# A tile that outlives its stage receives the next stage's first weight piece, and GpSimd clears the convolution input

## The reference, cut to what matters

```python
def first_block(x, c, ctx, c_ctx, ...):
    mx = split(silu(c) @ w_ada + b_ada, 6)          # shifts, scales and gates for the tokens
    mc = split(silu(c_ctx) @ w_ada + b_ada, 6)      # and for the 256 context tokens
    hx = modulate(rms_norm(x, g_pre_mix), mx[0], mx[1])
    hc = modulate(rms_norm(ctx, g_pre_mix), mc[0], mc[1])
    # token mixer: one projection (q, k, v, o, gates, ga, gb); a bidirectional mLSTM over q, k, v;
    # a depthwise convolution of width 31 over u = ga * sigmoid(gb); both @ w_out
    yx = token_mixer(hx, hc, w_in, ..., w_out)
    x = x + mx[2] * rms_norm(yx, g_post_mix)
    x = x + mx[5] * rms_norm(moe_ffn(...), g_post_ffn)      # 64 experts, 8 of them per token, one shared
    return x

def second_block(x, ...):
    for layer in range(2):
        h = rms_norm(x, norm[layer])
        x = x + (even_mixer(h, w_in, w_out) if layer == 0 else diff_mixer(h, w_qkv, ..., w_out))
        x = x + conv_ffn(rms_norm(x, ffn_norm[layer]), w_up[layer], conv_w, conv_b, w_down[layer])
    return rms_norm(x, final_norm)
```

## Time and profile before

| | |
|---|---|
| runs (median of three) | 2587.68 us (2585.64 to 2591.24) |
| profiled execution | 2594.0 us, its span 2592.2 us, around it 1.8 us |
| mean granted TensorE clock | 0.951 |
| busy PE, PEld | 2358.1 us (91%), 1759.2 us (68%) |
| busy DVE, ACT, POOL | 1536.8 us (59%), 1174.2 us (45%), 298.9 us (12%) |
| pieces of `w_in`, issue to landing, median | 3.2 us (20 of 512 KB) |
| pieces of `w_out`, issue to landing, median | 4.8 us (8 of 512 KB) |
| parts of the attention weights, issue to landing, median | 6.7 and 6.2 us (3 of 512 KB, twice) |
| quarters of the first `w_up` piece, issue to landing, median | 4.3 us (8 of 256 KB) |

### The profile page before, as it was taken

The page is one execution under the profiler, slowest core; times in us unless marked ns, Lnnn a source line. Parts: engine busy times, 40 slices in busy tenths (PEclk is TensorE's granted clock), DMA queues, the critical chain, the costliest instruction groups (busy, mean ns, idle before and its releaser), DMA issues. The chain is left out here.

```text
span 2592.2 us, 30584 instructions
## 1 busy us (share of the span) xinstructions
PE 2358.1 (91%) x10686; PEld 1759.2 (68%) x10686; DVE 1536.8 (59%) x2415; ACT 1174.2 (45%) x1853; POOL 298.9 (12%) x222
## 2 busy tenths in 40 slices
PE   6998887899999999982899789999989979999997
PEld 2875674576776776752666568888757757788886
DVE  3974445677777777748454447637536544674663
ACT  3314342566666666643354434324324533442341
POOL 0000000111211211220343000000014410000000
PEclk9997888999999999996999899999989999999999
DMA  6303424699999999956421212222232211323222
GB/s 241 104 25 123 147 74 166 235 360 359 351 356 357 358 353 354 375 214 239 162 73 41 74 67 96 93 102 97 82 130 73 66 29 52 130 89 103 89 85 72
DMA packets 87041, 427.39 MB, mean 165 GB/s; under 512 B 19760, under 2 KB 19888, under 8 KB 51344
## 3 DMA queue, kind: packets, MB, share of 16 engines
q1 hardware_dynamic: 67632, 392.32, 41.5%
q0 software_dynamic: 19296, 33.60, 3.6%
HBM read 415.36 MB, written 38.80 MB: 175 GB/s over the span
## 5 line engine op out<-in xcount | busy, mean ns | idle before, releaser
L1772 DVE TENSOR_TENSOR w_gu_low<-raw,w_gu_high 128x1024 fp32r<-128x1024 f32 x264 | 322.8, 1224 | 120.7 <-ACT w_gu_high L1721 106.8
L1721 ACT ACTIVATE w_gu_high<-raw 128x1024 fp32r<-128x1024 f32 x264 | 279.8, 1061 | 107.6 <-PE banks L1677 106.8
L2672 PE MATMUL banks<-h_high,w_high 128*128 128x512 f32 x704 | 275.8, 392 | 14.5 <-DVE w_low L2772 14.5
L2672 PE MATMUL banks<-h_low,w_high 128*128 128x512 f32 x704 | 275.3, 391 | 0.0
L2672 PE MATMUL banks<-h_high,w_low 128*128 128x512 f32 x704 | 275.3, 391 | 0.0
L1689 PE MATMUL banks<-raw,act_t 128*128 128x512 f32 x528 | 237.6, 593 | 0.9 <-ACT act_t L1744 0.9
L1677 PE MATMUL banks<-w_gu_high,x_t_high 128*128 128x512 f32 x528 | 213.5, 404 | 2.0 <-DVE x_t_low L1779 2.0
L1677 PE MATMUL banks<-w_gu_high,x_t_low 128*128 128x512 f32 x528 | 207.5, 393 | 0.0
L1677 PE MATMUL banks<-w_gu_low,x_t_high 128*128 128x512 f32 x528 | 207.1, 392 | 0.0
L2699 ACT ACTIVATE w_high<-raw 128x2048 fp32r<-128x2048 f32 (+2 forms) x74 | 124.1, 1676 | 156.4 <-PE banks L2682 152.7
L2736 DVE TENSOR_TENSOR w_low<-raw,w_high 128x2048 fp32r<-128x2048 f32 (+2 forms) x74 | 148.3, 2004 | 58.7 <-ACT w_high L2699 58.6
(11 more groups left out here) (443 smaller groups left out, 4710.6 us busy)
## 6 DMA issues: line engine op xcount, KB each, us to landing
raw<-in_w_e SPq DMA_DIRECT2D x198, 1024.0 KB, 9.5
raw<-in_w_up SPq DMA_DIRECT2D x42, 1024.0 KB, 4.8
w_ada<-in_w_ada_later SPq DMA_DIRECT2D x16, 1024.0 KB, 5.0
expert_rows<-y_rows SPq DMA_DIRECT2D x16, 1024.0 KB, 11.5
raw<-in_w_down SPq DMA_DIRECT2D x16, 768.0 KB, 4.2
w_qkv<-in_w_even SPq DMA_DIRECT2D x7, 1536.0 KB, 6.4
w_qkv<-in_w_odd SPq DMA_DIRECT2D x7, 1536.0 KB, 6.8
w_in<-in_w_in SPq DMA_DIRECT2D x20, 512.0 KB, 3.2
```

What stands on the lines that cost most here:

```text
L1721: act.activation(w_gu[c].high[:].rearrange("p j n -> p (j n)"), ex.chunk(c, s), ACT.Copy).then_inc(gu_high, 1)
L1772: dve.tensor_tensor(w_gu[c].low[:].rearrange("p j n -> p (j n)"), ex.chunk(c, s), w_gu[c].high[:].rearrange("p j n -> p (j n)").bitcast(F3 ...
L2672: mm = pe.matmul(ps[:, 2 * s + c, :], wp[:, at:at + P], hp[:, k, :], start=(k == 0 and i == 0), stop=(k == KT - 1 and i == 2))
```

## The change

A class `Early` holds one tile of 512 KB with a semaphore of its own, opened outside the stages; `fetch` asks for a transfer into it and counts, `now` gives the semaphore's value after the last one. Each of eight stages finds its first piece there, asked for by the stage ahead. Where the stage has a ring of four `raw` buffers, the early tile takes the place of the first. ACT and DVE treat the first piece ahead of the slices of `h`, where they did it after some. `u` is cleared by GpSimd. In `mlstm` the last eight rows reuse the place of the first eight. One `Early` serves from `prologue` to `mixer_out` and is closed after it, a second one serves from `combine` to the end.

```diff
+class Early:
+
+    def __init__(self, sb, sem):
+        self.tile, self.arrived, self.asked = sb("early", [P, KT * P]), sem("early_in"), 0
+
+    def fetch(self, sp, src):
+        sp.dma_start(self.tile[:], src).then_inc(self.arrived, 16)
+        self.asked += 1
+
+    def now(self):
+        return 16 * self.asked
...
                 sp.dma_start(m.rowv[:], d["rowv"]).then_inc(rowv_in, 16)
+                m.early.fetch(sp, d["w_in"][0])
                 sp.wait_ge(rowv_in, 16)
...
-        raw = [sb(f"w_in{s}", [P, KT * P]) for s in range(RAW)]
+        raw = [m.early.tile] + [sb(f"w_in{s}", [P, KT * P]) for s in range(1, RAW)]
+        first_here = m.early.now()
...
-                for p in range(len(PIECES)):
+                for p in range(1, len(PIECES)):
...
+            @block.gpsimd
+            def _(pool):
+                pool.memset(u[:], 0.0).then_inc(u_cleared, 1)
...
+                high(0)
                 for k in range(KT):
                     high_h(k)
-                    if k == 3:
-                        high(0)
...
-                own(dve, dve.memset(u[:], 0.0))
+                low_w(0)
                 for k in range(KT):
                     low_h(k)
-                    if k == 3:
-                        low_w(0)
...
+                dve.wait_ge(u_cleared, 1)
                 read(0)
...
 def mlstm(m, d, mix):
...
-            return early_rows[:, n, :] if n < N_LATER // 2 else late_rows[:, n - N_LATER // 2, :]
+            return kept_rows[:, n % (N_LATER // 2), :]
...
                     sp.dma_start(aw[n % SLOTS][:].rearrange("p k n -> p (k n)"), d["w_ada_later"][n]).then_inc(aw_in[n % SLOTS], 16)
+                m.early.fetch(sp, d["w_out"][:, 0:D])
...
 def mixer_out(m, d, src):
...
-                for k in range(KT):
+                for k in range(1, KT):
...
-                    act.wait_ge(raw_in[k % 4], 16 * (k // 4) + 16)
+                    if k == 0:
+                        act.wait_ge(m.early.arrived, first_here)
+                    else:
+                        act.wait_ge(raw_in[k % 4], 16 * (k // 4) + (16 if k % 4 else 0))
...
-def combine(m, scratch, gain, name, at):
+def combine(m, scratch, gain, name, at, following):
...
+                m.early.fetch(sp, following)
...
-def mix_out(m, w_dram, src, name, at, heads):
+def mix_out(m, w_dram, src, name, at, heads, following):
...
-                for j in range(KT):
+                for j in range(1, KT):
                     if j >= 4:
                         sp.wait_ge(w_low, j - 3)
                     sp.dma_start(raw[j % 4][:], w_dram[j]).then_inc(raw_in[j % 4], 16)
+                sp.wait_ge(w_low, 5)
+                m.early.fetch(sp, following)
...
-                    high(0)
+                high(0)
+                if heads:
                     high(1)
                 for k in range(KT):
                     if heads:
                         act.wait_ge(normed, k + 1)
                     act.activation(h.high[:, k, :], src[:, k, 0:SEQ], ACT.Copy).then_inc(h_high, 1)
-                    if k == 2 and not heads:
-                        high(0)
...
-def attention(m, d, w_name, o, diff):
+def attention(m, d, w_name, o, diff, following):
...
-                sp.dma_start(rope[:].rearrange("p a t -> p (a t)"), d["rope"]).then_inc(rope_in, 16)
-                for part in range(3):
+                for part in (1, 2):
                     sp.dma_start(w[0][:, part].rearrange("p k n -> p (k n)"),
                                  d[w_name][0][:, part * KT * P:(part + 1) * KT * P]).then_inc(first_in[part], 16)
+                    if part == 1:
+                        sp.dma_start(rope[:].rearrange("p a t -> p (a t)"), d["rope"]).then_inc(rope_in, 16)
                 sp.dma_start(amask[:].rearrange("p a t -> p (a t)"), d["amask"]).then_inc(amask_in, 16)
                 sp.dma_start(weights(1), d[w_name][1]).then_inc(w_in[1], 16)
+                sp.wait_ge(low_done, 1)
+                m.early.fetch(sp, following)
                 swap(0)
...
+                def high_first():
+                    act.wait_ge(m.early.arrived, first_here)
+                    act.activation(ws[0].high[:].rearrange("p k n -> p (k n)"), m.early.tile[:], ACT.Copy).then_inc(high_done, 1)
...
-                for part in range(3):
+                high_first()
+                for part in (1, 2):
                     act.wait_ge(first_in[part], 16)
                     high_part(0, 0, part)
                 act.wait_ge(w_in[1], 16)
...
-def conv_ffn(m, d, layer, name, at, room):
+def conv_ffn(m, d, layer, name, at, room, following):
...
+        def front(q):
+            return m.early.tile[:, quarter(q)] if q < 2 else raw[0][:, quarter(q)]
...
-                            for q in range(4):
-                                sp.dma_start(raw[0][:, quarter(q)], d["w_up"][layer][0][:, quarter(q)]).then_inc(front_in[q], 16)
+                            for q in (2, 3):
+                                sp.dma_start(raw[0][:, quarter(q)], d["w_up"][layer][0][:, quarter(q)]).then_inc(front_in[q - 2], 16)
                             load(0, 0, 1, 1, 1, True)
+                            if following is not None:
+                                sp.wait_ge(front_low, 2)
+                                m.early.fetch(sp, following)
...
 def program(nc, d, out, scratch):
...
+            s3, sb3, sem3 = m.open()
             s2, sb2, _ = m.open()
+            m.early = Early(sb3, sem3)
...
             mixer_out(m, d, mix)
+            s3.close()
...
-            s2, sb2, _ = m.open()
+            s2, sb2, sem2 = m.open()
             with s2:
                 m.hs, m.rstd = Split(sb2, "h", [P, KT, SEQ]), sb2("rstd", [P, SEQ])
+                m.early = Early(sb2, sem2)
```

More of the change, by code:

```diff
@@ L527, in high @@
                 def high(p):
-                    act.wait_ge(raw_in[p % RAW], 16 * (p // RAW) + 16)
+                    if p == 0:
+                        act.wait_ge(m.early.arrived, first_here)
+                    else:
+                        act.wait_ge(raw_in[p % RAW], 16 * (p // RAW) + (16 if p % RAW else 0))
                     if p >= SPLIT:
@@ L1157, in mixer_out @@
     with stack:
-        raw = [sb(f"w_out{s}", [P, D]) for s in range(4)]
+        raw = [m.early.tile] + [sb(f"w_out{s}", [P, D]) for s in range(1, 4)]
+        first_here = m.early.now()
         w, h = Split(sb, "w", [P, KT, D]), Split(sb, "h", [P, KT, SEQ])
@@ L2067, in mix_out @@
     with stack:
-        raw = [sb(f"w_out{s}", [P, KT * P]) for s in range(4)]
+        raw = [m.early.tile] + [sb(f"w_out{s}", [P, KT * P]) for s in range(1, 4)]
+        first_here = m.early.now()
         w = [Split(sb, f"w{s}", [P, KT * P]) for s in range(2)]
@@ L2087, in high @@
                 def high(j):
-                    act.wait_ge(raw_in[j % 4], 16 * (j // 4) + 16)
+                    if j == 0:
+                        act.wait_ge(m.early.arrived, first_here)
+                    else:
+                        act.wait_ge(raw_in[j % 4], 16 * (j // 4) + (16 if j % 4 else 0))
                     if j >= 2:
@@ L2129, in _ @@
                     dve.wait_ge(head_ready, 2)
-                    low(0)
+                low(0)
+                if heads:
                     norm(0)
@@ L2521, in low_part @@
                     dve.wait_ge(high_done, part + 1)
-                    dve.tensor_tensor(ws[part].low[:], w[0][:, part], ws[part].high[:].bitcast(F32), ALU.subtract).then_inc(low_done, 1)
+                    of = m.early.tile[:].rearrange("p (k n) -> p k n", k=KT) if part == 0 else w[0][:, part]
+                    dve.tensor_tensor(ws[part].low[:], of, ws[part].high[:].bitcast(F32), ALU.subtract).then_inc(low_done, 1)
                 low_part(0)
@@ L2585, in conv_ffn @@
         gate = [room[:, s, :] for s in range(2)]
-        raw_in, front_in = [sem("raw_in0"), sem("raw_in1")], [sem(f"front_in{q}") for q in range(4)]
+        raw_in, front_in = [sem("raw_in0"), sem("raw_in1")], [sem(f"front_in{q}") for q in range(2)]
         front_high, front_low, rstd_done = sem("front_high"), sem("front_low"), sem("rstd_done")
@@ L2718, in _ @@
                 for q in range(4):
-                    act.wait_ge(front_in[q], 16)
-                    act.activation(w[0].high[:, quarter(q)], raw[0][:, quarter(q)], ACT.Copy).then_inc(front_high if q < 3 else high_done, 1)
+                    act.wait_ge(*((m.early.arrived, first_here) if q < 2 else (front_in[q - 2], 16)))
+                    act.activation(w[0].high[:, quarter(q)], front(q), ACT.Copy).then_inc(front_high if q < 3 else high_done, 1)
                 in_pairs(act, job)
@@ L2771, in _ @@
                     dve.wait_ge(*((front_high, q + 1) if q < 3 else (high_done, 1)))
-                    dve.tensor_tensor(w[0].low[:, quarter(q)], raw[0][:, quarter(q)], w[0].high[:, quarter(q)].bitcast(F32),
+                    dve.tensor_tensor(w[0].low[:, quarter(q)], front(q), w[0].high[:, quarter(q)].bitcast(F32),
```

(12 more changed lines are left out.)

8 lines of the change are left out of this document (4 added, 4 removed).

## The result

The changed kernel takes 2571.18 us (median of 7 runs, 2564.65 to 2575.74) against 2591.24 us for the kernel before on the same chip. The ratio is 0.992, with a 95% interval of 0.9906 to 0.9934: 20 us, or 0.8%, faster. One of the seven runs of the kernel before took 3558.68 us and counts as a slow one; without it the median is 2590.58 us. The forecast was 2566.3 us with a range of 2559 to 2574 us and 21.4 us of gain.

The account below looks back on a forecast made before the run. PE, busy 91% of the span, was taken as the bound. First pieces 20.7, attentions 1.7, additions -1.0 gave 21.4 us off the median 2587.68 us: 2566.3 us, range 2559 to 2574 us.

Parts of the forecast that it names:

- The first piece, six stages: At the starts of `project_in`, `mixer_out`, both `mix_out` and both `conv_ffn`, PE begins earlier: 20.7 us gained together.
- The margin of the second piece: In the six stages the second piece is ready before PE finishes the first, with about 1 us to spare at the tightest.
- The two attentions: q starts earlier, ACT waits for the 1536 KB, k gains 2.95 and 3.55 us, the clock costs 4.8: 1.7 us gained.
- one is gone from ahead of it: 1243.1: In layer 0's `attention`, one 512 KB transfer fewer lets the 1536 KB land 1.45 us earlier, at 1243.1 instead of 1244.6.
- The other bound of that step: In `attention`, the 1536 KB land not earlier at all, if `mix_out`'s fetch right behind is served together with them.
- The price of the clock: In each `attention`, the hole of some 4 us makes k start at 1.2 GHz: 2.4 us each, 4.8 together.
- The rival in which the clock stays up: The clock stays up through the hole between q and k: 4.8 us more gain, 2561.5 us; chance 0.12.
- the rival of late transfers: First half: 1536 KB land no earlier; second: second piece late in `mixer_out`, `conv_ffn`. Up to 5.8 us lost, 2572.1; chance 0.14.
- What is added: Two closings of `Early`, each a clearing and a barrier, cost 1.0 us; the fetches and GpSimd's clearing of `u` cost nothing.
- The sum: Whole kernel: 20.7 + 1.7 - 1.0 = 21.4 us gained, giving a median of 2566.3 us.
- The last rival, that the fall of the clock only moves: Shorter holes give each stage a longer start at 1.2 GHz; not faster, 2587.7 us; chance 0.04.

Follow-up runs that it names:

- x5: The changed kernel with `project_in` asking for its own first piece at its start, the seven other handovers kept: 2571.36 us, ratio 0.9926 to the kernel before.
- x3: The changed kernel with the fetch of `mix_out`'s first piece in `attention` placed behind the first pair's swaps: 2569.19 us, ratio 0.9922 to the kernel before.
- x1: The changed kernel with both `attention` stages asking for q's weights themselves, the six other handovers kept: 2571.61 us, ratio 0.9931 to the kernel before.
- x6: The changed kernel with GpSimd clearing `u` twice, one after the other: 2571.93 us, a single run.
- x2: The changed kernel with ACT's wait for the second pair's weights moved behind taking out q's product: 2563.59 us, ratio 0.9903 to the kernel before.
- x7: The changed kernel with every barrier behind a clearing of semaphores doubled, 17 more barriers: 2575.85 us, ratio 0.9946 to the kernel before.
- x4: The changed kernel with the second pair's weights asked for ahead of `amask`, ACT's wait unmoved: 2559.51 us, ratio 0.9898 to the kernel before.
- x8: The changed kernel with the edits of x2 and x4 together: 2554.5 us, ratio 0.9855 to the kernel before; run again, 2559.17 us, 0.9878.
- the change's second one: The changed kernel run again, unaltered, beside the others: 2571.39 us, ratio 0.9934 to the kernel before.
- x9: The changed kernel with both edits of x8, but `attention` asking for q's weights itself as in x1: 2575.72 us, ratio 0.9943 to the kernel before.

## Why the prediction was right, and where it was off

**The first piece, six stages: right.** From start to first product, measured against predicted: `project_in` 4.05 (4.15), `mixer_out` 3.49 (3.55), `mix_out` of layer 0 2.52 (2.6), `conv_ffn` 3.64 (3.65) and 4.01 (4.15). `mix_out` of layer 1 gained 3.2 us (2.6): the hole of 2.57 us is gone, and the granted clock, low for 3.4 us behind that hole before, stayed up. The sum is 20.9 us where 20.7 was said. The margin of the second piece held: PE had no hole behind the first piece in `mixer_out` or `conv_ffn`. x5 shows by itself that the handover is the cause in one of the six; in the others the rows show it, and they weren't undone one by one.

**The two attentions: the mechanism right, its gain mis-sized.** The hold at the 1536 KB, the hole between q and k (4.49 and 4.41 us, some 4 predicted) and the fall of the clock all came. What failed is the step "one is gone from ahead of it: 1243.1": k started 2.10 and 2.66 us earlier, not 2.95 and 3.55, and over the five profiles of this code 2.15 and 2.79 us on average, with a spread from 1.4 to 4.2. Why it is less stays open. The other bound of that step, the fetch being served together with the 1536 KB, is what x3 points to in layer 0 without showing it, and in layer 1 no run tells. The price of the clock was 2.83 and 1.31 us, 4.1 together where 4.8 was said; over the five profiles it was 4.65 on average. Left is 0.6 us instead of 1.7 in the first profile, and from -1.5 to +3.1 us, 0.3 on average, over the five. x1 too shows that it can't be told from nothing. The rival in which the clock stays up is refuted by the rows at 0.65 and 0.81. Of the rival of late transfers the first half is open, with k 0.85 and 0.89 us later than forecast, and the second half is false.

**What is added: nearly right.** The hole of PE at the end of `mixer_out` grew from 10.19 to 10.59 us by the first closing, and from DVE's first row in `finish_out` to the end of the span it took 12.18 us instead of 11.81: two closings of 0.4 us each, where 1.0 was said. GpSimd's clearing took 2.60 us for 3008 columns, 0.86 ns a column; the estimate of 5.4 us from the row of 36 by 512 was twice too long. `w_low` is recorded with 1.52 us instead of 1.22 beside it, and none of that came through: from the start of ACT's copy to PE it took 3.07 us, and 3.06 us in x5, where the clearing was over. The prediction was right here on thin ground: in the earlier trace rows the subtraction overlapped the clearing for 0.43 of its 0.95 us only. The Trainium skill's rule in "GPSIMD Engine Reference", section Specifications, by which DVE instructions with two SBUF inputs contend with GpSimd, does not show in DVE's subtractions beside a clearing (x6). It does show beside GpSimd's subtractions in x2, which read SBUF: 2.05 and 2.74 us for 0.69. That is the limit which the Trainium skill's "SBUF — State Buffer", Who interferes with whom, draws, and this case agrees with it.

**The sum.** 20.9 + 0.6 - 0.8 = 20.7 us by the rows, and 20 us between the medians of the first comparison, 14.6 in the second, where 21.4 was forecast. That the rows and the first comparison agree so closely is partly luck: of the kernel before there is one profile, with `mlstm` at 101 us, and how often either kernel takes 93 or 101 us there isn't known. The predicted 2566.3 us is 5 us too low although the gain is off by 1 only: the three runs of the kernel before that were known had a median of 2587.68 us, the seven of the comparison 2591.24. The last rival, that the fall of the clock only moves, came only in traces. From the first product to the start of the next stage it took 55.17 us in `mix_out` of layer 0 (55.38 before) and 373.22 us in `conv_ffn` of layer 0 (373.24 before). In `mixer_out` it took 73.82 us (73.14 before, 0.4 of the difference being the closing), and in `conv_ffn` of layer 1 371.72 us (371.44 before). Those 0.3 us each go with a longer start at the low level, 5.3 us instead of 4.2 and 3.4 instead of 2.9.

## What to carry to other kernels

A first piece that is there at the start is worth its transfer only as far as the next wait on the same path: look at what takes the first result out, and at what that engine waits for before it does. If the early start opens a hole further on, count the hole and the clock behind it; if the wait can be moved behind the taking out, that edit can bring nothing alone and everything together with the early piece, so try the two together. Where a single profile and the median differ by more than the effect, compare stage by stage, and leave out stages that the change doesn't touch.

## What the runs showed that I had not expected

- `mlstm` took 92.5 to 101.3 us in thirteen executions, in steps, with PE's mean granted clock from 0.81 down to 0.75. A third of the difference between the first two profiles was this. In the five executions of 101 us, the kernel before among them, the granted clock was at 0.50 from 33 to 40 us and from 50 to 60 us after the start of the stage; in the two of 96.5 us only the first of these stretches was low, and in the five of 92.5 to 93 us neither; x7, with 100.2 us, has low stretches at other places. Why a given execution goes one way was not found.
- A DVE instruction on a tile of 128 by 2 took 2.58 us in the record beside GpSimd's clearing (0.17 us before), and ended with it, in each of the variants whose start I read (x5, x6, x7). What followed on DVE was not late by it. Whether the write or only its report is late stays open.
- A copy on DVE with one input was held too: `mask_now` took 2.21 us in x4 beside GpSimd's subtraction, and 0.43 us in the change with GpSimd idle.

```profile
1893.27 2.40 POOL L2586 TENSOR_TENSOR w_q_low<-w_qkv,w_q_high 128x1024 fp32r<-128x1024 f32 x1
1893.74 2.21 DVE L2575 COPY mask_now<-amask 128x512 f32<-128x512 f32 x1 [3.91 <-DMA amask<-in_amask]
```

- SP's asking for one transfer, 0.43 us as a rule, took 2.0 to 2.6 us in layer 1's attention in three of the profiles (the change, x3, x4) and in layer 0's in x5, and 0.4 to 0.7 us in layer 1 of x2, x8 and the change's second one. In layer 0 of x1 and x9 three transfers took 3.13 and 3.24 us to ask for, where 1.37 stood before, and in layer 1 of x9 2.83 us. The cause stays open.
